# Head norms' inverse roots by GpSimd's iteration, and another order of latent attention's query chunks

## The reference, cut to what matters

```python
def rms_norm(x, g):
    xf = x.astype(jnp.float32)
    y = xf * lax.rsqrt(jnp.mean(xf * xf, axis=-1, keepdims=True) + EPS)
    return (y * g.astype(jnp.float32)).astype(x.dtype)
...
    q = rms_norm(q, q_g)
    k = rms_norm(k, k_g)
    q = jnp.concatenate([q[..., :MLA_NOPE], apply_rope(q[..., MLA_NOPE:], pos)], axis=-1)
    k = jnp.concatenate([k[..., :MLA_NOPE], apply_rope(k[..., MLA_NOPE:], pos)], axis=-1)
...
        logits = jnp.einsum('bhqd,bhkd->bhqk', qb, k_t).astype(jnp.float32) * scale
        logits = jnp.where(allowed[None, None], logits, NEG_INF)
        probs = jax.nn.softmax(logits, axis=-1).astype(v_t.dtype)
        return jnp.einsum('bhqk,bhkd->bhqd', probs, v_t)
```

## Time and profile before

| | us |
|---|---|
| median of three runs | 2970.58 (2965.74 to 2973.03) |
| profiled execution, its own time | 2988.82 |
| its span, first to last instruction | 2987.5 |
| TensorE busy | 2875.9 (96%) |
| VectorE busy | 1858.2 (62%) |
| ScalarE busy | 1204.7 (40%) |
| GpSimd busy | 68.9 (2%) |

### The profile page before, as it was taken

How to read it: one execution, slowest core, us unless ns; L and a number is a source line. 1 busy time by engine, 2 the same in 40 slices (tenths; PEclk the granted TensorE clock), 3 DMA queues, 4 the chain that set the end, 5 groups by cost and what they waited for, 6 DMA issues and landing times.

```text
span 2987.5 us, 36065 instructions
## 1 busy us (share of the span) xinstructions
PE 2875.9 (96%) x14312; PEld 2407.0 (81%) x14312; DVE 1858.2 (62%) x2615; ACT 1204.7 (40%) x1810; POOL 68.9 (2%) x44
## 2 busy tenths in 40 slices
PE   8999999999999999999999977899999999999998
PEld 6888878887788888888778856788887888888887
DVE  4148766625766666666641277577457777777774
ACT  3144454634433323334331265776433333333432
POOL 0002210010000000000000000000000000000000
PEclk9999997999999999999999988888999999999999
DMA  4111220032211111113121100000211111111122
GB/s 169 50 36 57 79 99 1 6 123 78 106 56 50 51 57 52 50 54 127 50 92 57 37 14 10 22 1 1 92 43 42 50 57 57 47 53 57 56 93 85
DMA packets 47831, 172.99 MB, mean 58 GB/s; under 512 B 5648, under 2 KB 6160, under 8 KB 47664
## 3 DMA queue, kind: packets, MB, share of 16 engines
q1 hardware_dynamic: 47664, 170.68, 17.1%
HBM read 145.23 MB, written 25.43 MB: 57 GB/s over the span
## 4 chain that ended last, share of the span: by engine, by line
PE 87%; DVE 8%; ACT 3%; issue 2%; DMA 0%; SPq 0%; DVEq 0%; ACTq 0%
PE PS L295 14%; PE PS L297 14%; PE PS L299 14%; PE PS L1598 8%; PE PS L1599 8%; PE PS L1600 8%; PE PS L483 2%; PE PS L485 2%; PE PS L484 2%; PE PS L1186 2%; PE PS L706 2%; PE PS L1156 1%; PE PS L1171 1%; PE PS L3118 1%; DVE H L2790 1%
## 5 line engine op out<-in xcount | busy, mean ns | idle before, releaser
L289 DVE TENSOR_TENSOR w_lo<-w_raw,w_hi 128x1024 fp32r<-128x1024 f32 x93 | 117.1, 1262 | 203.1 <-ACT w_hi L283 203.1
L1598 PE MATMUL PS<-u_hi_f,w_hi 128*128 128x512 f32 x624 | 242.7, 389 | 0.0
L1599 PE MATMUL PS<-u_lo_f,w_hi 128*128 128x512 f32 x624 | 242.7, 389 | 0.0
L1600 PE MATMUL PS<-u_hi_f,w_lo 128*128 128x512 f32 x624 | 242.7, 389 | 0.0
L1547 ACT ACTIVATE w_hi<-weight_sums 128x512 fp32r<-128x512 f32 x156 | 98.1, 629 | 356.0 <-DVE weight_sums L1568 197.1
L283 ACT ACTIVATE w_hi<-w_raw 128x1024 fp32r<-128x1024 f32 x93 | 97.6, 1054 | 263.4 <-PE PS L485 136.5
L295 PE MATMUL PS<-f_ah,w_hi 128*128 128x512 f32 x640 | 197.1, 389 | 0.1
L297 PE MATMUL PS<-f_al,w_hi 128*128 128x512 f32 x640 | 197.0, 389 | 0.0
L299 PE MATMUL PS<-f_ah,w_lo 128*128 128x512 f32 x640 | 197.0, 389 | 0.0
L1553 DVE TENSOR_TENSOR w_lo<-w_raw,w_hi 128x512 fp32r<-128x512 f32 x205 | 137.3, 688 | 92.9 <-ACT w_hi L1547 92.9
L1598 PE MATMUL PS<-f_T_hi,w_hi 128*128 128x512 f32 x468 | 182.8, 390 | 1.9 <-issue 1.9
(11 more groups left out here) (447 smaller groups left out, 6612.4 us busy)
## 6 DMA issues: line engine op xcount, KB each, us to landing
w_raw<-in_weights SPq DMA_DIRECT2D x215, 512.0 KB, 3.6
H<-in_x_t SPq DMA_DIRECT2D x16, 512.0 KB, 4.3
h_kept<-H SPq DMA_DIRECT2D x16, 512.0 KB, 5.1
H<-h_kept SPq DMA_DIRECT2D x16, 512.0 KB, 6.7
stick_kept<-stick_stage SPq DMA_DIRECT2D x12, 512.0 KB, 2.8
mixer<-stick_kept SPq DMA_DIRECT2D x9, 512.0 KB, 6.8
p_kept<-p_stage SPq DMA_DIRECT2D x8, 512.0 KB, 4.0
p_pp<-p_kept SPq DMA_DIRECT2D x8, 512.0 KB, 8.1
```

The costliest lines, as they stand in the source:

```text
L289: dve.tensor_tensor(self.w_lo[i][:], self.w_raw[i][:], self.w_hi[i][:].bitcast(F32), ALU.subtract).then_inc(*self.s("w_lo").up(g))
L1598: pe.matmul(out, hi[:, self.chunk(k)], rh, start=opens and k == 0, stop=False, skip_group_check=True)
L1599: pe.matmul(out, hi[:, self.chunk(k)], rl, start=False, stop=False, skip_group_check=True)
L1600: mm = pe.matmul(out, lo[:, self.chunk(k)], rh, start=False, stop=k == 3, skip_group_check=True)
```

## The change

The square roots leave ScalarE. VectorE, right after the sums, computes the mean plus epsilon and a first guess of the inverse root from the bits of the number (`dve_rsqrt_start`, three small operations), and GpSimd refines it by three rounds of Newton's iteration (`pool_rsqrt`, twelve small operations, each waiting for the one before). VectorE then waits for GpSimd where it took the reciprocal. GpSimd's program gets `pool_norms`, the sixteen norms in the order in which they are needed. And `mla_item` takes the chunks of every head in the order 4, 3, 5, 2, 6, 1, 7, 0.

```diff
+        root = lambda name, n, offset: at(name, [P, 3, n], 4096 * 54 + offset)
+        self.df_root, self.out_root, self.mla_root = root("df_root", 4 * TT, 0), root("out_root", TT, 512), root(
+            "mla_root", 2 * TT, 1024)
...
+    def dve_rsqrt_start(self, tag, sums, tmp, dim):
+
+        dve, step = self.nc.vector, self.s("norm_guess")
+        mean, bits, guess = (tmp[:, i] for i in range(3))
+        dve.tensor_scalar(mean, sums, 1.0 / dim, EPS, ALU.mult, ALU.add).then_inc(*step.up(tag, "mean"))
+        dve.wait_ge(*step.at(tag, "mean"))
+        dve.tensor_scalar(bits.bitcast(I32), mean.bitcast(I32), 1, None, ALU.logical_shift_right).then_inc(
+            *step.up(tag, "half"))
+        dve.wait_ge(*step.at(tag, "half"))
+        dve.tensor_scalar(guess.bitcast(I32), bits.bitcast(I32), RSQRT_BITS, -1.0, ALU.subtract, ALU.mult).then_inc(
+            *step.up(tag, "guess"))
+
+    def pool_rsqrt(self, tag, out, tmp):
+
+        pool, step = self.nc.gpsimd, self.s("norm_rsqrt")
+        mean, square, guess = (tmp[:, i] for i in range(3))
+        pool.wait_ge(*self.s("norm_guess").at(tag, "guess"))
+        for n in range(3):
+            pool.tensor_tensor(square, guess, guess, ALU.mult).then_inc(*step.up(tag, n, "square"))
+            pool.wait_ge(*step.at(tag, n, "square"))
+            pool.tensor_tensor(square, square, mean, ALU.mult).then_inc(*step.up(tag, n, "product"))
+            pool.wait_ge(*step.at(tag, n, "product"))
+            pool.tensor_scalar(square, square, -0.5, 1.5, ALU.mult, ALU.add).then_inc(*step.up(tag, n, "correction"))
+            pool.wait_ge(*step.at(tag, n, "correction"))
+            if n < 2:
+                pool.tensor_tensor(guess, guess, square, ALU.mult).then_inc(*step.up(tag, n, "guess"))
+                pool.wait_ge(*step.at(tag, n, "guess"))
+            else:
+                pool.tensor_tensor(out, guess, square, ALU.mult).then_inc(*step.up(tag))
...
+    def pool_norms(self):
+        for h in range(DIFF_H):
+            self.pool_rsqrt(("diff", h), self.flat(self.df_norms), self.df_root)
+        for h in range(MLA_H):
+            self.pool_rsqrt(("mla", h), self.flat(self.mla_norms), self.mla_root)
+            if 0 <= h - 2 < DIFF_H:
+                self.pool_rsqrt(("diff out", h - 2), self.df_out_norm[:], self.out_root)
...
+    MLA_ORDER = (4, 3, 5, 2, 6, 1, 7, 0)
+
     def mla_item(self, n):
-        h, t = n // TT, n % TT
-        return h, t if h % 2 == 0 else TT - 1 - t
+        return n // TT, self.MLA_ORDER[n % TT]
...
-        act.wait_ge(*self.s("mla_sums").at(h, 0))
-        self.act_root(("mla", h), self.mla_norms[:], self.mla_norms[:], MLA_QK)
         yield
...
         dve.tensor_reduce(norms[:, 0, :], xq3, AX.X, ALU.add).then_inc(*sums.up(h, 0))
+        dve.wait_ge(*sums.at(h, 0))
+        self.dve_rsqrt_start(("mla", h), self.flat(norms), self.mla_root, MLA_QK)
         yield
         if h:
             yield
-        self.dve_rinv(("mla", h), norms[:])
-        dve.wait_ge(*self.s("rinv").at(("mla", h)))
+        dve.wait_ge(*self.s("norm_rsqrt").at(("mla", h)))
```

More of the change, by code:

```diff
@@ L11 @@
 U8 = mybir.dt.uint8
+I32 = mybir.dt.int32
+RSQRT_BITS = 0x5F3759DF
 ACT = mybir.ActivationFunctionType
@@ L2438, in diff_item, with flat @@
         return h, t if h % 2 == 0 else TT - 1 - t
+    def flat(self, norms):
+        return norms[:].rearrange("p a b -> p (a b)")
+    def pool_norms(self):
[5 more added lines that the diff above has]
+                self.pool_rsqrt(("diff out", h - 2), self.df_out_norm[:], self.out_root)
     def groups(self, ap, c=64):
@@ L2516, in act_diff_norms @@
         yield
-        act.wait_ge(*self.s("df_squares_summed").at(h))
-        self.act_root(("diff", h), self.df_norms[:], self.df_norms[:], 64)
-        yield
     def act_diff_parts(self, h):
@@ L2541, in dve_diff_norms @@
                 summed.then_inc(*self.s("df_squares_summed").up(h))
+                dve.wait_ge(*self.s("df_squares_summed").at(h))
+                self.dve_rsqrt_start(("diff", h), self.flat(self.df_norms), self.df_root, 64)
             yield
         yield
-        self.dve_rinv(("diff", h), self.df_norms[:])
-        dve.wait_ge(*self.s("rinv").at(("diff", h)))
+        dve.wait_ge(*self.s("norm_rsqrt").at(("diff", h)))
         for n in range(2):
@@ L2572, in act_diff_normed @@
         yield
[L2573 to L2576, removed]
     def dve_diff_normed(self, h):
@@ L2584, in dve_diff_normed @@
             *self.s("df_out_summed").up(h))
+        dve.wait_ge(*self.s("df_out_summed").at(h))
+        self.dve_rsqrt_start(("diff out", h), self.df_out_norm[:], self.out_root, P)
         yield
         yield
-        self.dve_rinv(("diff out", h), self.df_out_norm[:])
-        dve.wait_ge(*self.s("rinv").at(("diff out", h)))
+        dve.wait_ge(*self.s("norm_rsqrt").at(("diff out", h)))
         o3 = self.groups(self.res[:, h, :], P)
@@ L3322, in pool_program @@
         self.pool_out1()
+        self.pool_norms()
 def build_program(nc, known, a, gains_at, out):
```

## The result

| | before | change |
|---|---|---|
| median, runs side by side | 2969.09 | 2999.20 (2982.40 to 3000.97, 5 runs) |
| profiled execution, its span | 2987.5 | 2998.7 |
| ScalarE busy | 1204.7 | 1171.6 |
| VectorE busy | 1858.2 | 1863.4 |
| GpSimd busy | 68.9 | 116.3 |

What follows compares the result with a forecast made beforehand. It took latent attention's steps to be bound by a chain over VectorE and ScalarE, not by TensorE. Its terms summed to -4.4 us, added to the median of 2970.6: 2966 us, range 2954 to 2986.

Steps and rivals of the forecast that it cites:

- Wait for the root and reciprocals: Latent attention, heads 0 to 6: VectorE's wait for the root goes, -2.4 us, and its reciprocals of the roots, -2.8.
- part 6: Latent attention: GpSimd's twelve dependent operations take 0.25 us each, 3.0 in all, and are hidden, cost 0.
- Small operations: Latent heads 0 to 6: three small VectorE operations behind the sums, 0.5 us a norm, eleven norms, +5.5 us.
- VectorE's wait for the products goes: Latent attention: the new order ends VectorE's waits for TensorE's products after large chunks, -5.1 us, bounds 0 and -5.1.
- Hidden blocks: Latent steps 0, 2 and 3: nine more blocks where VectorE's work covers the exponential, 0.107 us each, -1.0 us.
- Table loads: ScalarE: 22 table loads, 28 us, and the square roots leave, worth nothing beyond the wait for the root.
- The rival on it: GpSimd is late: from 0.26 us an operation VectorE waits; at 0.40, +18 us, total 2984; chance 0.18.
- The last head: Latent attention's last head: TensorE owes fewer products and transposes at its start, -1.7 us, bounds 0 and -3.4.
- Head 0 at once: Latent head 0, prepared with nothing hiding it: 0.5 + 3.0 us instead of 2.4, +1.1, bounds +0.2 and +6.6.
- Head 0 at 1.2 GHz: Latent head 0: TensorE at half clock now meets larger chunks, +2.0 us, bounds 0 and +5.
- Differential attention: Differential attention: a reciprocal less and three small operations more for each of three heads, 0, bounds -1 and +1.5 us.
- the clock falling inside each head: Rival: TensorE falls to 1.2 GHz, slowing steps 2 to 4 in four latent heads, +10 us, total 2976; chance 0.14.

Runs made afterwards that it cites:

- the order alone: The kernel before with only the new order of chunks, roots still on ScalarE and VectorE: median 2969.75 us, ratio 0.9999 to before.
- two rounds: The change with the first of the three Newton rounds on GpSimd left out: median 2968.52 us, ratio 0.9995 to before.
- the late product: The change with a differential output's product and norm two steps later, step 4 instead of 2: median 2971.28 us, ratio 1.0009 to before.
- the second series: The change, unchanged, run again beside the kernel before: median 2983.04 against 2968.13 us, ratio 1.0043.

## Why the prediction was wrong, point by point

Its claim that a step is a chain over VectorE and ScalarE, 0.89 + 0.24 a block, or 2.12 + 0.24 with a part, held: without a fall of the clock the steps of four, two and seven blocks are 1.85, 2.60 and 3.80, on the line, and only that of one block, behind eight, is 1.31 instead of 1.13. The 22 loads and 33 us of ScalarE went, and were worth nothing, as said.

The sum was -4.4 us and the change cost some +15 where the first block ran alike, so the sign was wrong before the first block's stretch came on top.

1. *Wait for the root and reciprocals, -5.2.* The reciprocals went. The wait did not: 1.3 + 4.9 for GpSimd stand in its place, since part 6 failed.
2. *Small operations, +5.5.* 0.62 to 0.65 a norm instead of 0.5, about +7. A mis-sized term, not a wrong one.
3. *VectorE's wait for the products goes, -5.1.* **This step failed.** With the order alone the wait fell to 3.2, and a wait for scores of 4.4 stood beside it; in the change they are 3.8 and 5.4. Heads 0, 5 and 6 of the change are 0.15 to 0.4 us shorter than before, all parts together.
4. *Hidden blocks, -1.0*: too small to be told apart. 5. *Table loads*: right.
6. *GpSimd's chain, 3.0 us and hidden.* **This step failed, twice.** The rival on it had the right side and even the right threshold (0.26): an operation takes 0.30. By its formula, though, 0.30 would have cost 0.4 us in three heads, 0.5 in four and 0.6 in head 0, together 4. The rest came from where the prediction looked and turned away: the 1.80 us row was called a disturbance, and VectorE was said to read mostly PSUM in that stretch. The restaging reads two tiles of SBUF. Of the change's 192 operations 9 took 0.7 us or more, and each of them ran beside a VectorE operation with two SBUF inputs: eight beside restaging, one (1.07 us) beside a product of differential attention; more than thirty lay beside maxima out of PSUM and took 0.2. The two stretched ones, 0.54 + 0.57 longer, are the wait of 1.2. The Trainium skill (SBUF - State Buffer, Who interferes with whom) says just this: a VectorE instruction with two SBUF inputs contends with a GpSimd instruction that reads SBUF, and the second to start is blocked until the first is done. The nine rows agree, with the order of the starts known to some 0.02 us (at 2011.56 the operation held up is the one recorded first). One operation of the 192 does not: it started 0.03 us after such a VectorE operation and kept its 0.25 us, in the change's second profile too.

```profile
1771.72 1.36 DVE L2819 SCALAR_TENSOR_TENSOR H<-H,df_small 128x1024 f32<-128x1024 f32 x1
1771.75 0.25 POOL L385 TENSOR_TENSOR df_norms<-df_root 128x32 f32<-128x32 f32 x1
```

   The profile before already had the case: the 1.80 us operation of the earlier trace rows, at 256.76, and the two others as long start 0.04 us after a VectorE product that reads two SBUF tiles:

```profile
256.72 0.69 DVE L924 TENSOR_TENSOR mixer<-H,mixer 128x512 f32<-128x512 f32 x1 [0.41 <-PE PS L737]
```

   A prediction that had counted the SBUF inputs could have had the 1.1 us.
7. *The last head, -1.7*: -1.45. Right.
8. *Head 0 at once, +1.1.* +3.3: the chain 1.8, and 1.6 from a fall of the clock that the prediction had no term for.
9. *Head 0 at 1.2 GHz, +2.0.* -0.4 in the change, +1.1 with the order alone. TensorE's stand before the third item of head 0 was 5.4 us where it had been 5.95 before, and began 1.5 us later, and the clock fell later as well: at 1918.8 instead of 1914.9, until 1925.7 instead of 1932.0.
10. *Differential attention, 0.* -3.4 in the first pair of profiles, but the unchanged kernel was itself at 333.0 once and at 328.8 once, and the seven profiles with GpSimd's roots lie from 329.5 to 332.5, so nothing of it is credited to the change.

**The largest term was a rival held at 0.14**: the clock falling inside each head. It foresaw the four heads, and +10; it was 8.5. Its reason was half wrong. It named the heads with a differential output for their long idle stretch, which held; but it priced steps 2 to 4, and the loss came in steps 5 and 6, and it laid the fall to small chunks between large ones, while with the order alone only heads 3 and 6 fell behind head 0. What TensorE stood still for was VectorE, in a step 2 of 5.6 us that ends in a wait for GpSimd; with that step shortened (two rounds) or its work moved (the late product) the same order cost little or nothing. Filled with repeated work, TensorE kept its clock though the wait stayed. So two rivals that were priced apart were one event: the wait costs 4.5 us directly and pulls 8.5 of the clock behind it, together 13 of the 14.1 that heads 1 to 4 lose; the small operations, less what the reciprocals and the order gave back, are the rest. The range would have held the 2983 of the second series; the first block's stretch, which the prediction met as an unexplained 18 us between profile and runs, took the recorded median to 2999.

Left open: what decides the clock in the first block's stretch and in differential attention, and why the change's falls within latent attention repeat to 0.1 us between two profiles while those do not, nor the kernel before's own in heads 2 and 4.

## What to carry to other kernels

A wait added to one engine is to be priced with what stands still behind it: here 1.2 us on VectorE cost some 3 us a head, because TensorE lost its clock over it, and filling the gap with useless matmuls gave 2 of them back. Before small work goes to GpSimd, count the SBUF inputs of what VectorE does meanwhile, and take 0.3 us for each dependent operation. Work on the engine that carries the chain is free only where that engine waits: the sum and the product of an output cost 2.4 us in steps 0 and 2, and nothing and 0.3 us beside exponentials of eight and seven blocks.

## What had not been expected of the hardware

A GpSimd operation on 8, 16 or 32 elements takes about the same when each waits for the last: 0.28, 0.30 and 0.32 us from start to start. Dependent small operations on VectorE follow each other every 0.21 us. Beside a VectorE operation with two SBUF inputs such a GpSimd operation took 0.74 to 1.07 us instead of 0.20 to 0.25. An unchanged stretch of 45 us ran at 1.2 or at 2.4 GHz from one execution to the next, 16 us apart, more than most changes to this kernel are worth.
